# Two norm borders of a transformer kernel: a weight half split in quarters on two engines, modulation moved, squares tile by tile

## The reference

```python
def sublayer(h, i, fn, resid_w):
    shift, scale, gate = mod[:, i, 0], mod[:, i, 1], mod[:, i, 2]
    u = rms_norm_2(h, norm_pre[l, i]) * (1.0 + scale) + shift
    return h + resid_w * gate * rms_norm_2(fn(u), norm_post[l, i])

h = sublayer(h, 0, lambda u: swiglu(u, ffn1_w_gate[l], ffn1_w_up[l], ffn1_w_down[l]), 0.5)
h = sublayer(h, 1, lambda u: token_mixer(u, w_in[l], ...), 1.0)
h = sublayer(h, 2, lambda u: swiglu(u, ffn2_w_gate[l], ffn2_w_up[l], ffn2_w_down[l]), 0.5)
```

## Time and profile before

| | |
|---|---|
| median of three runs | 1302.83 us |
| profiled execution | 1301.58 us, span 1299.9 us |
| TensorE matmuls | 1289.5 us busy, 99% of the span |
| VectorE | 954.3 us, 73% |
| ScalarE | 625.3 us, 48% |
| GpSimd | 62.3 us, 5% |
| TensorE's granted clock in both borders | 1.00 of full speed |

### The profile page before, as it was taken

The page is one execution under the profiler, slowest core; times in us unless marked ns, Lnnn a source line. Parts: engine busy times, 40 slices in busy tenths (PEclk is TensorE's granted clock), DMA queues, the critical chain, the costliest instruction groups (busy, mean ns, idle before and its releaser), DMA issues.

```text
span 1299.9 us, 27403 instructions
## 1 busy us (share of the span) xinstructions
PE 1289.5 (99%) x11150; PEld 1248.0 (96%) x11150; DVE 954.3 (73%) x1246; ACT 625.3 (48%) x744; POOL 62.3 (5%) x102
## 2 busy tenths in 40 slices
PE   9999999999999999999999999999999999999998
PEld 9988899999999999999999999999999899999986
DVE  7666788887577866888875788766977667877744
ACT  6356554344354355534443544443645665544433
POOL 3000000000003000000000000000011000000000
PEclk9999999999999999999999999999999999999999
DMA  7642266566755434556576588676485334576543
GB/s 279 208 134 89 103 199 222 194 217 212 237 179 191 138 124 148 201 202 209 198 252 216 192 275 280 216 248 231 162 267 208 132 135 166 174 233 222 180 166 125
DMA packets 40405, 252.32 MB, mean 194 GB/s; under 512 B 4544, under 2 KB 4800, under 8 KB 16144
## 3 DMA queue, kind: packets, MB, share of 16 engines
q1 hardware_dynamic: 29232, 211.89, 47.2%
q0 software_dynamic: 10816, 39.32, 9.6%
q10 hardware_dynamic: 288, 0.13, 0.0%
HBM read 250.27 MB, written 1.05 MB: 193 GB/s over the span
## 4 chain that ended last, share of the span: by engine, by line
PE 86%; DVE 5%; ACT 4%; DMA 2%; issue 2%; POOL 0%; DVEq 0%; SPq 0%; ACTq 0%; POOLq 0%
PE ps L2222 70%; PE ps L2929 4%; DVE w_lo L1125 2%; ACT w_hi L493 2%; PE ps L2253 2%; DMA raw<-in_units_ffn_up 1%; PE ps L2474 1%; PE ps L2604 1%; ACT scratch L712 1%; PE ps L2653 1%; PE ps L2707 1%; DMA scratch<-in_const_mix 1%; PE ps L2319 0%; PE ps L2351 0%; PE ps L2904 0%
## 5 line engine op out<-in xcount | busy, mean ns | idle before, releaser
L2222 PE MATMUL ps<-x_hi,w_hi 128*128 128x258 f32 (+2 forms) x2016 | 577.2, 286 | 1.1 <-DVE w_lo L1125 0.8
L2222 PE MATMUL ps<-x_hi,w_lo 128*128 128x258 f32 (+2 forms) x2016 | 571.1, 283 | 0.0
L493 ACT ACTIVATE w_hi<-raw 128x2048 fp32r<-128x2048 f32 (+1 forms) x178 | 352.7, 1981 | 414.1 <-PE ps L2222 311.5
L2222 PE MATMUL ps<-x_lo,w_hi 128*128 128x258 f32 (+2 forms) x1856 | 527.7, 284 | 0.0
L1125 DVE TENSOR_TENSOR w_lo<-raw,w_hi 128x2048 fp32r<-128x2048 f32 (+1 forms) x177 | 420.2, 2374 | 121.3 <-ACT w_hi L493 120.1
L2222 PEld LDWEIGHTS ps<-x_hi,w_hi 128*128 128x128 f32 x2016 | 380.2, 189 | 7.5 <-issue 3.7
L2222 PEld LDWEIGHTS ps<-x_hi,w_lo 128*128 128x128 f32 x2016 | 380.8, 189 | 0.0
L2222 PEld LDWEIGHTS ps<-x_lo,w_hi 128*128 128x128 f32 x1856 | 350.1, 189 | 0.2
L2222 PE MATMUL ps<-g_hi,w_hi 128*128 128x256 f32 (+1 forms) x576 | 162.9, 283 | 0.0
L2222 PE MATMUL ps<-g_hi,w_lo 128*128 128x256 f32 (+1 forms) x576 | 162.7, 282 | 0.0
L2222 PE MATMUL ps<-g_lo,w_hi 128*128 128x256 f32 (+1 forms) x576 | 162.4, 282 | 0.0
(11 more groups left out here) (396 smaller groups left out, 1649.6 us busy)
## 6 DMA issues: line engine op xcount, KB each, us to landing
raw<-in_units_ffn_up SPq DMA_DIRECT2D x44, 1024.0 KB, 5.0
raw<-in_units_glu_up SPq DMA_DIRECT2D x44, 1024.0 KB, 5.2
v_tok<-in_w_ada_t POOLq DMA_DIRECT2D x72, 512.0 KB, 4.0
raw<-in_units_ffn_down SPq DMA_DIRECT2D x16, 1408.0 KB, 5.9
raw<-in_units_mix_in SPq DMA_DIRECT2D x20, 1024.0 KB, 5.0
raw<-in_units_hgrn_in SPq DMA_DIRECT2D x16, 1024.0 KB, 5.0
raw<-in_units_fox_in SPq DMA_DIRECT2D x14, 1024.0 KB, 5.0
raw<-in_units_glu_down SPq DMA_DIRECT2D x8, 1408.0 KB, 6.1
```

The costliest lines, as they stand in the source:

```text
L493: nc.scalar.activation(w_hi[s][:, 0:size], raw[s][:, 0:size], ACT.Copy).then_inc(hi_ready, 1)
L2222: ins = T_.matmul(dst, fixed, moving, start=(kt == 0 and i == 0), stop=(kt == kts - 1 and i == 2), skip_group_check=first)
```

## The change

At the two borders:

- The first half of unit 1 is copied by ScalarE in two quarters, the first ahead of the root and the second behind it. VectorE subtracts the first quarter, GpSimd the second (`second_quarter_lo`), for which its queue of modulation loads is cut in two at both places.
- The second half is copied by ScalarE behind all late tiles, where it stood ahead of them. VectorE's `second_half_lo` also waits for GpSimd's quarter. TensorE waits for that quarter at the third tile.
- `modulation_1`, with the shift columns now in it, runs ahead of the last tile of glu1_down, where it stood behind it; the shift columns stood between the first and the second tile of `post_and_pre`.
- In mix_out the last two tiles are squared and added one by one. TensorE signals the first of them when its column is done. VectorE adds the two rows of `sq_acc` and then the square of tile 6, so that `tile_sums` has two matmuls in place of four.
- Four semaphores are merged into two, with the same order of work.

```diff
+QUARTERS = (slice(0, UNIT // 4), slice(UNIT // 4, UNIT // 2))
...
+            def first_quarter_hi(name):
+                pair = GEMMS[name]["first"] // 2
+                act.wait_ge(raw_landed[1], pair * 16 + 16)
+                act.wait_ge(unit_done, pair * 2 + 2)
+                nc.scalar.activation(w_hi[1][:, QUARTERS[0]], raw[1][:, QUARTERS[0]], ACT.Copy).then_inc(half_hi, 1)
+
+            def second_quarter_hi():
+                nc.scalar.activation(w_hi[1][:, QUARTERS[1]], raw[1][:, QUARTERS[1]], ACT.Copy).then_inc(half_hi, 1)
...
+                    if width == 2 and type(it) is int and (it, s) == (1, 1):
+                        act.wait_ge(first_of_two, 2)
+                        nc.scalar.activation(sq[:, KD - 2:KD - 1, 0:SEQ], ps[:, 2:3, 0:SEQ], ACT.Square).then_inc(tile_sq, 1)
+                        read_wait(pair, s)
+                        nc.scalar.activation(sq[:, KD - 1:KD, 0:SEQ], ps[:, 3:4, 0:SEQ], ACT.Square).then_inc(tile_sq, 1)
+                        return
...
             gemm("glu1_down", tile_squares(1), defer=True)
-            first_half_hi("mix_in")
+            first_quarter_hi("mix_in")
             inverse_rms(5, SEQ)
-            second_half_hi()
+            second_quarter_hi()
             act.wait_ge(mod_ready, 2)
             late_tiles_hi(1, 1)
+            second_half_hi()
             next_halves_hi("mix_in")
...
+            def first_quarter_lo(n):
+                dve.wait_ge(half_hi, n)
+                V.tensor_tensor(w_lo[1][:, QUARTERS[0]], raw[1][:, QUARTERS[0]], w_hi[1][:, QUARTERS[0]].bitcast(F32), ALU.subtract).then_inc(half_lo, 1)
...
+            def modulation_1():
+                read_modulation(3, 26, 54)
+                pre_gain(1)
+                post_gain(1)
+                shift_columns(1)
+                dve.wait_ge(mod_set, 4)
+                V.memset(lam_tmp[:, 0:1], 0.0).then_inc(mod_ready, 1)
...
+                if type(it) is int and (it, s) == (1, 1):
+                    dve.wait_ge(sq_added, SQ_ADDED["mix_out"] + 2)
+                    V.tensor_tensor(sq_acc[:, 0, :], sq_acc[:, 0, :], sq_acc[:, 1, :], ALU.add).then_inc(sq_added, 1)
+                    for n, k in enumerate((KD - 2, KD - 1)):
+                        dve.wait_ge(tile_sq, TILE_SQ["mix_out"] + 4 + n)
+                        ins = V.tensor_scalar(y_raw[:, k, :], ps[:, 2 + n, 0:SEQ], mod_g[:, 1, k:k + 1], None, ALU.mult)
+                        if n == 0:
+                            dve.wait_ge(sq_added, SQ_ADDED["mix_out"] + 3)
+                            V.tensor_tensor(sq_acc[:, 0, :], sq_acc[:, 0, :], sq[:, k, 0:SEQ], ALU.add).then_inc(sq_added, 1)
+                    ins.then_inc(banks_free[1], 1)
                     return
...
-                if turn == 0:
-                    shift_columns(1)
...
+                dve.wait_ge(quarter_lo, turn + 1)
                 second_half_lo(name)
...
-            gemm("glu1_down", gained_tile(0, "glu1_down"), defer=True, ada="glu1_down")
-            modulation_1()
-            first_half_lo(3)
+            gemm("glu1_down", gained_tile(0, "glu1_down"), defer=True, ada="glu1_down", ahead_of_last=modulation_1)
+            first_quarter_lo(3)
             post_and_pre(5, 1, 0, "mix_in")
...
+            def second_quarter_lo(n):
+                pool.wait_ge(half_hi, (4, 7)[n - 1])
+                G.tensor_tensor(w_lo[1][:, QUARTERS[1]], raw[1][:, QUARTERS[1]], w_hi[1][:, QUARTERS[1]].bitcast(F32), ALU.subtract).then_inc(quarter_lo, 1)
...
-            load_modulation(ADA["hgrn_out"][0], ADA["glu2_up"][2] - ADA["hgrn_out"][0])
+            load_modulation(ADA["hgrn_out"][0], ADA["mix_in"][2] - ADA["hgrn_out"][0])
+            second_quarter_lo(1)
+            load_modulation(ADA["mix_in"][2], ADA["glu2_up"][2] - ADA["mix_in"][2])
...
+                                if kt == 2 and s == 1:
+                                    pe.wait_ge(quarter_lo, outer[2] + 1)
...
-            def tile_sums(name, width=1):
-
-                pe.wait_ge(sq_added, SQ_ADDED[name] + (KD if width == 1 else 2))
-                for w in range(width):
-                    T_.matmul(ps[:, 4, 0:SEQ], ones, sq_acc[:, w, :], start=(w == 0), stop=False)
-                pe.wait_ge(tile_sq, TILE_SQ[name] + KD // width)
-                for k in range(KD - width, KD):
-                    ins = T_.matmul(ps[:, 4, 0:SEQ], ones, sq[:, k, 0:SEQ], start=False, stop=(k == KD - 1))
-                ins.then_inc(norm_ss, 1)
+            def tile_sums(name, tiles):
+
+                pe.wait_ge(sq_added, SQ_ADDED[name] + tiles)
+                T_.matmul(ps[:, 4, 0:SEQ], ones, sq_acc[:, 0, :], start=True, stop=False)
+                pe.wait_ge(tile_sq, TILE_SQ[name] + tiles + (name == "mix_out"))
+                T_.matmul(ps[:, 4, 0:SEQ], ones, sq[:, KD - 1, 0:SEQ], start=False, stop=True).then_inc(norm_ss, 1)
```

More of the change, by code:

```diff
@@ L1079, in _ @@
             gemm("mix_out", tile_squares(2), defer=True)
-            first_half_hi("glu2_up")
+            first_quarter_hi("glu2_up")
             inverse_rms(7, SEQ)
-            second_half_hi()
+            second_quarter_hi()
             act.wait_ge(mod_ready, 3)
             late_tiles_hi(2, 2)
+            second_half_hi()
             next_halves_hi("glu2_up")
@@ L1329, in _ @@
             V.tensor_tensor(lb_tmp[0], l0, lb, ALU.subtract)
-            V.tensor_tensor(lb_tmp[1], l1, lb, ALU.subtract).then_inc(lb_shift, 1)
+            V.tensor_tensor(lb_tmp[1], l1, lb, ALU.subtract).then_inc(exp_inputs, 1)
             def first_tiles_lo(g):
@@ L1398, in _ @@
             steps.wait()
-            V.tensor_reduce(lam_tmp[0:1, 0:2], lam_in[0:1, 0::2, :], AX_X, ALU.add).then_inc(lam_sums, 1)
+            V.tensor_reduce(lam_tmp[0:1, 0:2], lam_in[0:1, 0::2, :], AX_X, ALU.add).then_inc(exp_inputs, 1)
             v_copy = normed_out(lambda it, s: proj1[:, bass.ds(it * 4 + (16 + 2 * s), 2), :])
@@ L2084, in _ @@
             gemm("mix_out", gained_pair, defer=True)
-            first_half_lo(5)
+            first_quarter_lo(6)
             post_and_pre(7, 2, 1, "glu2_up")
             sum_squares(6, SEQ)
-            next_halves_lo("glu2_up", 6)
+            next_halves_lo("glu2_up", 8)
             dve.wait_ge(norm_rstd, 9)
@@ L2176, in _ @@
             G.tensor_copy(fails_r[:], mix_raw[:, 8 * P:10 * P].rearrange("p (a b) -> p a b", b=P)).then_inc(mix_const, 1)
-            load_modulation(ADA["glu2_up"][2], 4)
+            load_modulation(ADA["glu2_up"][2], 1)
+            second_quarter_lo(2)
+            load_modulation(ADA["glu2_up"][2] + 1, 3)
         @block.tensor
@@ L2186, in _, with gemm @@
             pe.sem_inc(hq_ss, 1)
-            def gemm(name, xw, xh, xl, T, k=None, after=None, late=None, mid=None, packed=False, outer=None, resume=False, by_tokens=(), its=None):
+            def gemm(name, xw, xh, xl, T, k=None, after=None, late=None, mid=None, packed=False, outer=None, resume=False, by_tokens=(), its=None, first_tile=None):
                 g = GEMMS[name]
@@ L2235, in unit_pair @@
                                     ins.then_inc(unit_done, 1)
+                                elif first_tile and s == 1:
+                                    ins.then_inc(first_tile, 1)
                                 if mid:
@@ L2397, in spread_heads @@
                 pe.wait_ge(f_neg, 1)
-                pe.wait_ge(heads_set, 1)
+                pe.wait_ge(head_tables, 2)
                 pe.wait_ge(hq_rstd, g + 2)
@@ L2739, in _ @@
             gemm("glu1_down", from_hidden(2), gh, gl, SEQ)
-            tile_sums("glu1_down")
+            tile_sums("glu1_down", KD)
             keep_busy(7, 14)
@@ L2916, in _ @@
             ins.then_inc(unit_done, 1)
-            gemm("mix_out", None, gh, gl, SEQ, resume=4)
-            tile_sums("mix_out", 2)
+            gemm("mix_out", None, gh, gl, SEQ, resume=4, first_tile=first_of_two)
+            tile_sums("mix_out", 4)
             keep_busy(7, 12)
```

26 lines of the change are left out of this document (11 added, 15 removed).

## The result

The changed kernel takes 1305.28 us (median of 22 runs), the kernel before on the same chips 1301.95 us (22 runs): a ratio of 1.0025, 95% interval 1.0016 to 1.0033. It is slower by 3.3 us, where the prediction had +2.1 (1304.9, range 1301.7 to 1306.4). The profiled execution has a span of 1303.1 us.

What follows compares the result with a forecast made beforehand. TensorE, busy for 99% of the span, bounds the kernel, so only gaps can move. Late copy plus GpSimd slowdown, 0.41 + 0.6 and 0.50 + 0.6 us at the two borders, gave +2.1 us: median 1304.9, range 1301.7 to 1306.4.

Steps and rivals of the forecast that it cites:

- the forecast: Both borders: late half copy plus a 0.6 us GpSimd slowdown each, +2.1 us in all; chance 45%.
- full slowdown: Both borders: VectorE's two-input steps beside GpSimd lose 1.0 us in each, +2.9 us in all, 1305.7; chance 18%.
- Late half: VectorE's w_lo half waits for ScalarE's later copy: 0.41 us at glu1_down to mix_in, 0.50 at mix_out to glu2_up.
- GpSimd's hold: Both borders: VectorE slowed while GpSimd subtracts the second quarter, taken as 0.6 us each, delaying all late tiles.
- a loss of 0.45 us for each us of GpSimd's work: Rate from three VectorE adds beside GpSimd; times 1.8 us of GpSimd's quarter gives 0.8 us, taken as 0.6.
- 30 to 45% longer: Sign of being right: VectorE's steps beside GpSimd's subtract lengthen by this share.
- The bound of 1.0 from the earlier trace: Upper bound of VectorE's loss in a border: the whole 1.0 us of three adds beside GpSimd.
- Modulation ahead of the last tile: Glu1_down to mix_in: first sum 0.38 us later, second sum and first product 0.18; shift columns 0.29 off VectorE.
- its two bounds: Start of mix_in: end of the keep_busy matmuls and readiness of the first x_hi tile, said to coincide.
- Quarter ahead of the root: Glu1_down to mix_in: scale(0) starts right behind the root, 0.27 us earlier; TensorE gains nothing at the stage's start.
- Squares tile by tile: Mix_out to glu2_up: two of four sum matmuls go, but the others wait for VectorE; gain 0.08 us.
- Start of the stage: Mix_in's first product right behind the unchanged keep_busy matmuls, moving from 910.54 to 910.72; 28 and 24 keep_busy records stay.

Runs made afterwards that it cites:

- experiment 8: Changed kernel with ScalarE copying both quarters ahead of the root, so that GpSimd's subtract starts earlier; ratio 1.0011 to the kernel before.
- experiment 2: Changed kernel with ScalarE's second half of w_hi copied ahead of its late tiles again, GpSimd keeping its quarter; ratio 1.0006 to the kernel before.
- experiment 10: Changed kernel with both quarters on VectorE, ScalarE's second half copied behind its first x_hi tile and fewer keep_busy matmuls; ratio 1.0000 to the kernel before.
- experiment 7: Kernel before with only the modulation and its shift columns moved ahead of the last tile of glu1_down; ratio 1.0000.
- experiment 4: Kernel before plus two GpSimd two-input subtracts of 192 columns on an unread buffer in each border; one run, borders +1.00 us.
- experiment 5: Kernel before plus two GpSimd one-input copies of 192 columns on an unread buffer in each border; one run, borders +0.39 us.
- experiment 6: Kernel before with only the second quarter of w_lo moved to GpSimd, VectorE subtracting the first ahead of the root; ratio 1.0014.
- experiment 9: Changed kernel with GpSimd's subtract of 512 columns cut into four of 128; one run, borders +3.02 us against the kernel before.
- experiment 1: Changed kernel with the second quarter of w_lo subtracted by VectorE instead of GpSimd; ratio 1.0016 to the kernel before.

## Why the prediction was right, and where its size was off

The direction and both causes are those predicted. But by the prediction's own mark, a hold of more than 0.85 us in a border, it was not the forecast (45%) that was met but the rival called full slowdown (18%, +2.9 us). A change of over 2.6 us to the slower side had 27%, "the same" 67%. And that the predicted 1304.9 us lies so near the 1305.28 measured is luck: it starts from a median of three runs that was 0.9 us above the later one (1301.95), and the step from there was 1.2 us too short.

- **Late half.** Predicted 0.41 and 0.50 us against the kernel before. With the hold of 1.09 taken off, the changed kernel has 1.47 - 1.09 = 0.38 and 1.73 - 1.09 = 0.64 (measured without the hold in experiment 8, border 2: 0.66). The mechanism is the predicted one, idle VectorE time ahead of w_lo, reload and squares queued behind it; experiment 2 shows it. Undoing it gives back more than these terms, 1.00 and 0.96, as then VectorE also keeps what it won elsewhere: in border 1 scale(0) is 0.32 us earlier behind the last product, and the shift columns (0.29) are out of its way.
- **GpSimd's hold: the term that was mis-sized.** "As the short adds here have a fixed share that need not stretch, I take 0.6." It measured 1.09 in each border, 0.98 us more in all, nearly the whole difference between +2.1 and +3.2. The step that failed is the rate, a loss of 0.45 us for each us of GpSimd's work. VectorE's instructions are not slowed by a share of their length. One that starts beside GpSimd's is held until that ends, a short one as long as a long one, and the others keep their length; so the sign "30 to 45% longer" didn't show, but one instruction of 1.50 us in place of 0.42. The rows behind the rate say the same once they are read one by one. At 14.67 the third add alone takes 1.42 of the 3.11 us and ends 0.59 us behind GpSimd's subtract. The split at 418.39 starts when GpSimd has 0.51 us left, and loses 0.36. The other half of the product was off the other way: GpSimd's subtract took 1.44 us, not 1.8, since the row it was scaled from held a wait of GpSimd for VectorE's add. The bound of 1.0 from the earlier trace rows was the better value.
- **Modulation ahead of the last tile.** The sums came 0.29 and 0.19 us late against 0.38 and 0.18 predicted. The first product was not 0.18 late but 0.05 early. I had its two bounds as coinciding, but one lay a little behind the other. In the kernel before the first x_hi tile ends 4.33 us behind the last product, and the first product follows 0.14 us later. The same 0.14 to 0.15 us lie between them in border 2, in both borders of experiment 10, and in experiment 7. So the x_hi tile set the start, and the keep_busy matmuls could be 0.09 us later. It had no effect on the time, as experiment 7 shows.
- **Quarter ahead of the root.** scale(0) starts right behind the root in border 1 (0.03 us), as predicted, and TensorE gets nothing from it.
- **Squares tile by tile.** First sum in border 2 at 0.89 us behind the last product, where the matmul that waited for ScalarE stood at 0.99: 0.10 gained, 0.08 predicted. The two sum matmuls saved left a gap of 0.61 us. This part was not run alone.
- **Start of the stage.** First products at 4.42 and 4.64 against 4.47 and 4.73. In border 1 the first x_hi tile ends at 4.01, 0.32 us earlier than before, and the keep_busy matmuls, as many as before, cover it. In border 2 it ends at 4.50, 0.08 us earlier, and the first product follows it by 0.14 us as before.

The Trainium skill (SBUF — State Buffer, SBUF: two separate sides) says that the ports that VectorE and GpSimd share are an exclusive lock, not a split: whichever starts first has it for the whole instruction, and the other blocks. The runs agree: the add already running kept its 0.42 us, and scale(1) behind it ended 0.29 us after GpSimd's subtract. The price is not the whole length of GpSimd's instruction, as VectorE's earlier one still runs for the first part of it: two GpSimd subtracts of 0.58 and 0.57 us cost VectorE 0.61 in all. Against my 0.6 for the hold this rule was the better guide.

## What to carry to other kernels

Work that goes from VectorE to GpSimd is free only where VectorE starts nothing beside it that can be held: here a subtract of 512 columns cost VectorE 1.09 us, and doing it itself 0.6. The price is what is left of GpSimd's instruction when VectorE's next one starts, so look for a place where VectorE waits anyway. When a copy is moved out of one engine's critical place, look at who waits for its result at the new place, and what is queued behind the waiter (here the half, the squares, the reload). And where filler matmuls keep TensorE busy, a shorter chain beside them gives nothing until there are fewer of them.

## What the runs showed of the hardware

- A held VectorE instruction ends a fixed time behind GpSimd's. In the changed kernel and in experiments 2, 4, 5, 6, 8 and 9 there are 21 held instructions of 256 columns, and all end 0.27 to 0.29 us behind GpSimd's, whether that took 0.39 us or 1.45. The loss is what was left of GpSimd's instruction less 0.13 to 0.15 us (for the x_lo tiles, 0.47 us by themselves, less 0.2):

| run | GpSimd's instruction | left when VectorE's starts | lost |
|---|---|---|---|
| changed | subtract, 512 columns | 1.21 | 1.08 |
| experiment 8, border 1 | subtract, 512 | 0.51 | 0.36 |
| experiment 8, border 2 | subtract, 512 | 0.07 | 0 |
| experiment 4, border 2 | subtract, 192 | 0.44 | 0.31 |
| experiment 5, border 2 | copy, 192 | 0.29 | 0.15 |
| experiment 9, border 1 | subtract, 128 | 0.40 | 0.26 |

- It works the other way too. GpSimd's instruction ends a fixed time behind the VectorE instruction that ran when it started: 1.13 to 1.14 us with 512 columns, 0.36 to 0.37 with 192 and two inputs, 0.20 to 0.21 with 192 and one, 0.31 to 0.32 with 128. So its own time holds a wait. In the kernel before, a subtract of 136 columns that starts at 418.98 us behind VectorE's split takes 2.34 us, and ends 0.28 us after the split.
- Not every VectorE instruction is held. The cast with one input was. This one, which reads one input from PSUM (`ps`), starts in the kernel before when a GpSimd instruction has 0.57 us left, and takes the 0.69 to 0.70 us that it always takes:

```profile
416.44 0.69 DVE L1302 TENSOR_TENSOR proj<-ps,rstd 128x516 f32<-128x516 f32 x1 [1.17 <-PE ps L2222]
```

- A VectorE instruction already running when GpSimd starts keeps its length: add(0) at 909.38 took 0.42 us, though GpSimd's subtract started at 909.49.
- GpSimd's subtract of 512 columns took 1.27 us where VectorE's instruction ahead of it was over 0.12 us after its start (experiment 8), and 1.44 where that had 0.31 us to go (changed kernel).
- The gaps of up to 0.6 us left TensorE's clock alone: the granted clock is 1.00, the 2.4 GHz level, in both border stretches of the kernel before, of the changed one and of experiment 1.
